# A hybrid encoder trunk on one core: the 32-column gate tile leaves the ring of weight tiles and becomes sixteen plain fp32 matmuls in four column parts

## The reference

```python
h = rms_norm(x, p['norm_mix'][layer])
proj = h @ p['ev_w_in'][e]
u, q, k, v, og, glr = jnp.split(proj, EV_SPLITS, axis=-1)
y_s5 = s5_mixer(u, ...)            # bidirectional scan over 32 groups x 64 states
y_gla = gla_mixer(q, k, v, og, glr, ...)
# in gla_mixer
lr = glr.astype(f32).reshape(bsz, L, 2, GLA_RANK)
logit = jnp.einsum('blzr,zrk->blzk', lr, w_gate.astype(f32)) + b_gate.astype(f32)
g = (jax.nn.log_sigmoid(logit) / GLA_TAU).reshape(bsz, L, 2, GLA_HEADS, GLA_DK)
# after the mixer: memory cross-attention (256 memory tokens per group), then the MLP
m = rms_norm(mem, p['norm_mem'][layer])
```

## Time and profile before

| | us |
|---|---|
| median of 3 runs | 2384.88 (2384.05 to 2385.65) |
| the profiled execution, device time | 2384.38 |
| its span, first to last instruction | 2382.6 |
| PE busy | 2371.8 |
| DVE busy | 1554.5 |
| ACT busy | 1175.5 |

### The profile page before, as it was taken

How to read it: one execution, slowest core, us unless ns; L and a number is a source line. 1 busy time by engine, 2 the same in 40 slices (tenths; PEclk the granted TensorE clock), 3 DMA queues, 4 the chain that set the end, 5 groups by cost and what they waited for, 6 DMA issues and landing times.

```text
span 2382.6 us, 34363 instructions
## 1 busy us (share of the span) xinstructions
PE 2371.8 (100%) x13607; PEld 2010.3 (84%) x13607; DVE 1554.5 (65%) x2637; ACT 1175.5 (49%) x2080; POOL 0.2 (0%) x4
## 2 busy tenths in 40 slices
PE   9999999999999999999999999999999999999999
PEld 6988877888889888987788888888888898888887
DVE  8999768776477876664666438858985465433332
ACT  5334455555345565645464436646874453433432
POOL 0000000000000000000000000000000000000000
PEclk9999999999999999999999999999999999999999
DMA  5435632563124654443235223233334323333332
GB/s 203 107 95 157 223 111 84 177 207 122 62 89 148 196 186 134 138 135 106 74 96 169 96 89 124 89 107 98 98 98 151 117 86 118 122 97 98 98 97 89
DMA packets 109695, 291.28 MB, mean 122 GB/s; under 512 B 18944, under 2 KB 40576, under 8 KB 108256
## 3 DMA queue, kind: packets, MB, share of 16 engines
q1 hardware_dynamic: 100832, 264.83, 35.1%
q10 hardware_dynamic: 8704, 24.25, 3.3%
HBM read 267.45 MB, written 19.50 MB: 120 GB/s over the span
## 4 chain that ended last, share of the span: by engine, by line
PE 87%; DVE 2%; ACT 1%; issue 0%; ACTq 0%
PE ps L1558 64%; PE ps L1544 5%; PE ps L1581 3%; PE ps L1549 3%; PE ps L1697 2%; PE ps L1652 2%; PE ps L1677 2%; PE ps L1724 1%; PE ps L1712 1%; PE ps L1665 0%; PE ps L2121 0%; PE ps L2188 0%; PE ps L1597 0%; DVE wlo L1517 0%; PE ps L1614 0%
## 5 line engine op out<-in xcount | busy, mean ns | idle before, releaser
L1512 ACT ACTIVATE whi<-wraw 128x1024 fp32r<-128x1024 f32 x430 | 452.0, 1052 | 203.5 <-PE ps L1558 125.4
L1517 DVE TENSOR_TENSOR wlo<-wraw,whi 128x1024 fp32r<-128x1024 f32 x430 | 522.4, 1218 | 8.0 <-ACT whi L1512 7.8
L1558 PE MATMUL ps<-in_hP,whi 128*128 128x512 f32 x1272 | 506.2, 398 | 1.7 <-DVE in_lP L2018 0.9
L1558 PE MATMUL ps<-in_hP,wlo 128*128 128x512 f32 x1272 | 495.9, 390 | 0.0
L1558 PE MATMUL ps<-in_lP,whi 128*128 128x512 f32 x1272 | 495.3, 389 | 0.0
L1558 PE MATMUL ps<-hid_P,whi 128*128 128x512 f32 x1024 | 316.7, 390 | 0.0
L1558 PEld LDWEIGHTS ps<-in_hP,whi 128*128 128x128 f32 x1272 | 238.8, 188 | 57.9 <-issue 5.4
L1558 PEld LDWEIGHTS ps<-in_hP,wlo 128*128 128x128 f32 x1272 | 238.8, 188 | 50.8
L1558 PEld LDWEIGHTS ps<-in_lP,whi 128*128 128x128 f32 x1272 | 239.0, 188 | 49.1 <-issue 1.0
L1940 DVE TENSOR_TENSOR x<-ps,x 128x256 f32<-128x256 f32 (+1 forms) x192 | 106.8, 556 | 259.8 <-PE ps L1558 258.1
L1558 PE MATMUL ps<-in_S,whi 128*128 128x256 f32 x1408 | 261.3, 287 | 0.0
(11 more groups left out here) (527 smaller groups left out, 3671.7 us busy)
## 6 DMA issues: line engine op xcount, KB each, us to landing
wraw<-wt SPq DMA_DIRECT2D x432, 512.0 KB, 3.5
wraw<-wt ACTq DMA_DIRECT2D x17, 512.0 KB, 4.2
k_scratch<-region_P SPq DMA_DIRECT2D x16, 256.0 KB, 3.1
v_scratch<-vtmp SPq DMA_DIRECT2D x32, 128.0 KB, 3.5
x<-x_in SPq DMA_DIRECT2D x4, 768.0 KB, 6.8
x<-x_in SPq DMA_DIRECT2D x2, 1536.0 KB, 7.0
mix_mem<-mem_in ACTq DMA_DIRECT2D x1, 2048.0 KB, 15.9
region_S<-k_scratch ACTq DMA_DIRECT2D x2, 1024.0 KB, 7.2
```

The source lines that it names most:

```text
L1512: nc.scalar.activation(whi[:, (n + 3) % NHI, :, :], wraw[:, ws(n), :, :], ACT.Copy).then_inc(wh.sem, 1)
L1517: nc.vector.tensor_tensor(wlo[:, ws(n), :, :], wraw[:, ws(n), :, :], whi[:, (n + 3) % NHI, :, :].bitcast(F32), ALU.subtract).then_inc(wr.s ...
L1558: last = nc.tensor.matmul(ps[:, bank(m), 0:N[prod.g]], w_[:, k, :], x_[:, k, :], start=(k == 0 and j == 0), stop=(k == KT - 1 and j == 2))
```

## The change

1. The weight ring has 16 tiles instead of 17 (`NT_MIX = 16`), and `TILES = [(6,), (7, 8, 9), (10, 11, 12), (13, 14, 15)]`. One tile stands between `pe_bu(0)` and `pe_y(0)` instead of two; the other batches keep three each.
2. The 32 columns of `glr` get a small buffer `wlr` (128x8x32) with a DMA of its own. A new `pe_narrow` stands on PE between tile 0 and tile 1. It has 16 plain fp32 matmuls of 32 array columns; the eight slices of the sum over 1024 go in two rounds of four, each of the four to its own column part and its own 32 rows of PSUM.
3. The four partial sums stay apart. ACT copies all 128 rows out at once to `lr` (now 128 rows), the gate weights are repeated four times, and the gate matmul in the second block sums over 128 rows instead of 32. The DMAs of `lr` and `wgate` grow fourfold.
4. The copies to `qf`, `qr`, `nqi` and `cneg` go from DVE to ACT (`act_tables`, 11 activations between tile 0 and tile 1 of ACT's list). DVE waits for them ahead of `dve_vv(0)`.
5. `dve_mem_root` has two steps instead of three; a square by ACT and the use of -1 instead of 1 in the sum (`nones`, set on DVE at the start) take over the rest.
6. On DVE `dve_rot(0)` and `low(6)` stand ahead of `dve_rt(0)`, and `low(7)` leaves batch 0.

```diff
-NT_MIX = 17
+NT_MIX = 16
+            def pe_narrow(pe):
+
+                pe.wait_ge(bc_l.sem, 64)
+                for z, (lo, hi) in enumerate(((0, TP), (TP, T))):
+                    for kk in range(0, KT, 4):
+                        for q in range(4):
+                            last = nc.tensor.matmul(ps[32 * q:32 * q + 32, 2 + z, 0:hi - lo], wlr[:, kk + q, :], x[:, kk + q, lo:hi],
+                                                    start=(kk == 0), stop=(kk == KT - 4))
+                last.then_inc(ssum.sem, 1)
...
+            def act_tables(a):
+
+                for i, sign in enumerate((1.0, -1.0)):
+                    nc.scalar.activation(qf[0:NS, i, :, :], pw[0:NS, i, 1:SC + 1, :], ACT.Copy, scale=sign)
+                    nc.scalar.activation(qf[NS:P, i, ::-1, :], pw[NS:P, i, 1:SC + 1, :], ACT.Copy, scale=sign)
+                    nc.scalar.activation(qr[NS:P, i, :, :], pw[NS:P, i, 0:SC, :], ACT.Copy)
+                    nc.scalar.activation(qr[0:NS, i, ::-1, :], pw[0:NS, i, 0:SC, :], ACT.Copy)
+                nc.scalar.activation(nqi[NS:P, :, :], pw[NS:P, 1, 0:SC, :], ACT.Copy, scale=-1.0)
+                nc.scalar.activation(nqi[0:NS, ::-1, :], pw[0:NS, 1, 0:SC, :], ACT.Copy, scale=-1.0)
+                a.wait_ge(bc_l.sem, 64)
+                nc.scalar.activation(cneg[:, :, :], cc[:, 1], ACT.Copy, scale=-1.0).then_inc(setup.sem, 1)
...
-            TILES = [(6, 7), (8, 9, 10), (11, 12, 13), (14, 15, 16)]
+            TILES = [(6,), (7, 8, 9), (10, 11, 12), (13, 14, 15)]
...
                     high(a, 1)
...
-                    for n in range(4):
+                    act_tile(a, 0)
+                    a.wait_ge(ssum.sem, 2)
+                    nc.scalar.activation(lr[:, :], banks(2), ACT.Copy).then_inc(setup.sem, 1)
+                    act_tables(a)
+                    for n in range(1, 4):
                         act_tile(a, n)
...
                     dve_mem_root(v)
                     low(v, 3)
+                    v.wait_ge(setup.sem, 2)
                     dve_vv(v, 0)
...
-                    dve_rt(v, 0)
                     dve_rot(v, 0)
                     low(v, 6)
+                    dve_rt(v, 0)
                     dve_input(v, 0)
-                    low(v, 7)
                     dve_scan(v, 0)
```

More of the change, by code:

```diff
@@ L368, in pe_tile @@
                         for j, (w_, x_) in enumerate(((whi[:, n % NHI], in_h), (whi[:, n % NHI], in_l), (wlo[:, n % NRAW], in_h))):
-                            last = nc.tensor.matmul(ps[0:m, z, 0:hi - lo], w_[:, k, 0:m], x_[:, k, lo:hi],
+                            last = nc.tensor.matmul(ps[:, z, 0:hi - lo], w_[:, k, :], x_[:, k, lo:hi],
                                                     start=(k == 0 and j == 0), stop=(k == KT - 1 and j == 2))
@@ L712, in _ @@
                         pe.wait_ge(msq.sem, k + 1)
-                        last = nc.tensor.matmul(ps[:, 4, :], ones, early[k], start=(k == 0), stop=(k == KT - 1))
+                        last = nc.tensor.matmul(ps[:, 4, :], nones, early[k], start=(k == 0), stop=(k == KT - 1))
                     last.then_inc(msum.sem, 1)
-                    for n in range(4):
+                    pe_tile(pe, 0)
+                    pe_narrow(pe)
+                    for n in range(1, 4):
                         pe_tile(pe, n)
@@ L729, in _ @@
                     tile(6)
-                    tile(7)
                     pe_y(pe, 0)
@@ L1052, in trunk_tail @@
             gs = {g: {n: sig(f"{n}_{g}") for n in ("sqd", "sql", "acd", "ssum", "sroot", "snew", "an", "ah", "ar", "ap", "hx",
-                                                   "qad", "tqd", "vtr", "vcp", "vca", "kvl", "kad", "ksc")} for g in "PS"}
+                                                   "qad", "tqd", "vtr", "vcp", "vca", "kvl", "kad", "ksc")
+                      if g == "P" or n not in ("kad", "ksc")} for g in "PS"}
             gs["F"] = {n: sig(f"{n}_F") for n in ("sqd", "ssum", "sroot", "snew", "an")}
@@ L2707 @@
     by_token = w["od_w_in"][0][:, 2 * D:].reshape(4, 2, P, 2, 512).transpose(3, 0, 2, 1, 4).reshape(KT, P, KT * P)
-    wt = _np.concatenate([tiles(late[n]) if n != "din" else _np.concatenate([tiles(late[n])[:2 * KT], by_token], 0) for n in WT_ORDER], 0)
-    wgate = _np.zeros((2 * 16, 2, 256), _np.float32)
+    narrow = _np.zeros((1, P, KT * P), _np.float32)
+    narrow[0, :, :32 * KT] = glr_.reshape(KT, P, 32).transpose(1, 0, 2).reshape(P, 32 * KT)
+    parts = {n: tiles(late[n]) for n in WT_ORDER}
+    parts["ev"] = _np.concatenate([parts["ev"], narrow], 0)
+    wt = _np.concatenate([parts[n] if n != "din" else _np.concatenate([parts[n][:2 * KT], by_token], 0) for n in WT_ORDER], 0)
+    wgate = _np.zeros((4, 2 * 16, 2, 256), _np.float32)
     for z in range(2):
-        wgate[16 * z:16 * z + 16, z] = w["gla_w_gate"][0][z]
+        wgate[:, 16 * z:16 * z + 16, z] = w["gla_w_gate"][0][z]
+    wgate = wgate.reshape(P, 2, 256)
     j, i = _np.arange(P)[:, None], _np.arange(P)[None, :]
```

52 lines of the change are left out of this document (21 added, 31 removed).

## The result

| | before | after |
|---|---|---|
| median | 2384.23 us (2383.88 to 2385.65, 22 runs) | 2388.05 us (2387.25 to 2389.34, 22 runs) |
| ratio | | 1.0017, 95% interval 1.0010 to 1.0023 |
| span of the profiled execution | 2382.6 us | 2386.0 us |
| first block ends at | 232.32 us | 236.56 us |
| from there to the end | 2150.28 us | 2149.44 us |

The changed kernel is 3.8 us slower. The 95% interval of the ratio does not contain 1, so this is more than noise; it is still less than the 0.2% that the prediction set as its bound for calling a kernel slower. The forecast was 2388.6.

What follows compares the result with a forecast made beforehand. PE, without a hole through the first block, was taken as the bound. 2.8 - 1.14 - 0.24 + 0.06 + 2.2 = 3.7 us on 2384.38 gave 2388.1, plus 0.5 for the median: 2388.6 us; range 2385.0 to 2394.5.

Steps and rivals of the forecast that it cites:

- three signs of being wrong: Wait at `pe_y(0)` under 2 us, narrow tile over 5 us, or first block ending before 232.3.
- Narrow tile: Sixteen new PE matmuls between tiles 0 and 1, four parts at once: 2.8 us added, ends 2.5 and 10.1.
- The estimate from the Trainium skill: Narrow tile priced at the skill page's 0.79 per part: 3.2 us, making the sum 0.4 us higher.
- its two readings: Two prices for matmul parts side by side: a fixed 0.24 us per group, or the skill's 0.79 per part.
- The chain on DVE: Batch 0: PE's product reaches DVE at 87.47; without `low(7)`, 1.14 us less, states are ready at 104.1.
- The stand: PE ends tile 6 at 97.1 and waits 7.1 us for DVE's states before `pe_y(0)` at 104.2.
- The clock after the stand: `pe_y(0)` runs slowly after PE's idleness, 1.7 times as long for 5.4 us: 2.2 us lost, ends 0 and 2.7.
- The rival in which the clock holds: The stand leaves PE's clock alone, so only 1.5 us are added: 2386.4 us; chance 0.13.
- the one in which it stays low to tile 7: Half clock lasts from `pe_y(0)` until tile 7, 8.2 us more: 2394.6 us; chance 0.12.
- The loads of the second block: Fourfold `lr` and gate weight loads, issued by 232.67 and wanted at 237.98: no cost, 5.3 us of cover.
- ACT: Copy and 11 small activations behind the narrow tile: 5 us, from 39 to about 45, no cost, 2 us cover.
- The rival of the other side: DVE's scan input need not wait for PE, so `pe_y(0)` comes 5.2 us earlier: 2379.7 us; chance 0.06.

Runs made afterwards that it cites:

- the last experiment: Kernel before, 17 tiles, with `pe_bu(0)` moved ahead of tile 5 and `dve_rt(0)` inside the rotation table: 2392.96 us, ratio 1.0037.
- the filled stand: Changed kernel with 30 more matmuls of 512 columns, result unread, between tile 6 and `pe_y(0)`: 2384.87 us, ratio to before 1.0003.

## Why the prediction was right

The mechanism was right in each step on the path of the first block, and none of the three signs of being wrong appeared. That the sum came out within 0.6 us is in part luck: two errors cancel, the clock's price, which was set 0.6 us too low, and a gain in the second block that was not in the prediction.

- **Narrow tile.** Predicted 2.8, measured 2.72. Of the ends 2.5 and 10.1 the near one held. 2.72 is 2.53 and 0.19 on top, near the 0.24 us of `pe_lag(0)` that was read as a fixed price; no run here varies the length, so that the price is fixed is not shown. The estimate from the Trainium skill, 3.2, was too high: four parts with 512 and 256 columns ran 3.7 times as fast as the 10.13 us of tile 0, 0.93 per part. The prediction also put `pe_lag(0)` between its two readings, which is wrong: its 0.98 us are 0.75 per part (5.91 / 0.98 / 8), below the 0.79 and not between.
- **The chain on DVE.** Predicted: lag step at about 81, input at 87.47, states at 104.1. Measured 79.99 + 0.77, 87.50, 104.06 + 0.09. The removal of `low(7)` was worth its 1.1 us.
- **The stand.** Predicted 7.1, measured 6.86. `pe_y(0)` began when forecast; the view counts the wait from the modelled end of tile 6's last matmul, 97.35, and the prediction from where the next matmul would have started, 97.1.
- **The clock after the stand.** The step that was mis-sized: 2.2 predicted, 2.79 measured, just above the upper end of 2.7. The duration was good, 5.4 against 5.6 us. The factor was wrong. I had doubled only the column time of a matmul, which gave 1.7 times; the rows say 2, for 5.6 us at the lower level lost 2.79, half of them. The pairs of `pe_bu(0)` in the last experiment say nearly the same, 5.29 us for 2.79. How long the lower level lasts is less certain than this one execution makes it look: over the eight profiled executions with a stand the loss is between 2.09 and 3.24 us (see the open points). The rival in which the clock holds is refuted by the filled stand, the one in which it stays low to tile 7 by the stretch from 112 at 1.00. The rule of the Trainium skill ("TensorE: Matmul & The Clock Gate", "HAM oscillation — how this bites in real kernels"), that the burst behind a gap begins cold, was borne out here.
- **The loads of the second block.** Called free, with 5.3 us of cover for what was to land. The gate weights landed 5.4 us after their issue, where they had taken 1.9. The cover was gone, and the first gate group begins 0.48 us behind its predecessor and not 0.23, so 0.25 us. The kernel before with 128 rows loads the same bytes, `lr` in four pieces of 96 KB instead of one of 384; there the weights landed after 2.7 us and nothing waited for them.
- **The second block.** Not in the prediction at all: the gate matmuls over 128 rows are cheaper than those over 32. 1.21 us less by the kernel before with this part alone; less the 0.25 of the late load that is 0.96, near the 0.84 that the profile of the change shows.
- **ACT.** Predicted 5 us and done by 45, measured 5.0 us (39.13 to 44.2). The cover held.

In the sum: 4.24 us to the end of block one where 3.7 were forecast (0.6 of the clock), -0.84 in block two where 0 was, 3.4 in the spans and 3.8 in the medians. The time of 2388.6 was built on a median of 2384.88 from three runs; over 22 runs it is 2384.23, which is why the time missed by 0.55 us and the difference by 0.1. The rival of the other side, where DVE is not fed by PE, fell with the 6.74 us wait of L613.

What stays open:

- Why the wait of 1.2 us at 506 us appears in some versions.
- Why the lower clock cost so different amounts behind much the same stand. Behind seven stands of 6.86 to 6.91 us it cost 2.79 in the changed kernel, and 2.63, 3.04, 2.58, 3.24, 2.78 and 2.50 in the runs without the narrow tile, with one part, with the copies on DVE, with the lag step first, with the 32-row gates and with the early product in the kernel before. Behind the one of 6.24 us it cost 2.09.
- The 0.4 us by which block one of the kernel before moved between two executions with the same order (232.32 and 231.93), which is also how far a difference between single profiles can be trusted.

## What to carry to other kernels

When PE shows no waits, ask of each piece of work not what it costs but what it covers: a tile of 8.3 us taken out from between a product and its use brought a stand of 6.9 us and then a slow clock, and the same removal brought 5.1 us once the product had been put earlier. A cover can be moved instead of kept, but each engine on the chain must be early enough: in the kernel before, where DVE is later by its setup work and by the place of one small instruction, the early product cost 8.7 us. And a null result belongs to its schedule: the copies to ACT were worth nothing in one, and in the other DVE's last step ahead of the product came 4.3 us earlier, of which 3.1 are their length.

## What the runs showed of the hardware

- After a stand of 6.9 us TensorE's granted clock was at 0.50, and thin fp32 work of 96 columns ran at half speed for 5.6 us. Over eight such stands of 6.2 to 6.9 us the loss was 2.1 to 3.2 us. Thirty matmuls of 512 columns put into the stand kept it at 1.00.
- Four column parts of fp32 with 512 and 256 columns cost 2.72 us against 10.4 one after another, 0.96 per part.
- A group of four matmuls over 32 rows among matmuls over 128 cost 0.39 us more than the same group over 128 rows, although it reads a quarter of the data.
- A load of 256 KB landed 5.4 us after its issue behind one of 384 KB, and 2.7 us behind four of 96 KB.
